# Attention's gate projection on four column groups, and rotations of keys and queries one job later

## The chip, the cores and the metric

The kernel runs on one core of one Trainium2 chip. The metric is the device time of one execution in microseconds (us). Before the change the median of three runs is 1970.93 us (1968.88 to 1974.15).

## The reference, cut to what matters

Two layers of a hybrid model over 512 tokens of width 1024, all in fp32. Each layer normalises the tokens, multiplies them by one wide matrix, and feeds the pieces to three branches (attention with compressed, selected and window keys; a spatial gating unit; a state space model, S5), which are gated, summed and mixed. Then comes a mixture of 32 experts. What the change touches are the 24 columns of attention's gates and the rotary positions:

```python
h = rms_norm(x, norm_mix_g[l])
parts = jnp.split(h @ w_in[l], split_points, axis=-1)
q, k_c, v_c, k_s, v_s, k_w, v_w, nsa_g, sgu_in, s5_in, branch_g = parts     # nsa_g: 24 columns
nsa_gates = jax.nn.sigmoid(nsa_g.astype(jnp.float32)).reshape(B, S, G, R, 3)
...
q_rot = partial_rope(q, positions)
k_slc = partial_rope(k_slc, positions)
k_win = partial_rope(k_win, positions)
...
return gb[..., 0:1] * o_c + gb[..., 1:2] * o_s + gb[..., 2:3] * o_w          # gb: the gates of a block
```

## The kernel before, in words

Each layer is written out as one block with a hand-ordered program for each engine; engines meet through semaphores. A layer has three stages: the projections with S5 (some 145 us), attention with the branch gates and the mixing (some 355 us), and the experts (some 470 us).

TensorE's program of the first stage, in order (line numbers are the profile's):

- Four token jobs `token_job(t)` (L599), one for each tile of 128 tokens: 8 fp32 matmuls of 128x512, the spatial gating unit's input. Every fp32 matmul stands in the trace as two instructions, each with its own weight load, so a job is 16 of them. After job 1 come `nsa_job(0)` and `nsa_job(1)`, after jobs 2 and 3 come `nsa_job(2)` and `nsa_job(3)` (L591): the 24 gate columns of a token tile, 8 matmuls with the tile of `hT` (the turned, normalised tokens) as 128x128 stationary operand and 24 moving columns of `wnsa`. ScalarE takes the sums as tanh (L1134, `nsa_g`).
- Feature jobs (`feature_job`, L585): 24 matmuls of 128x512 in a single-pass type, fp32 split in a high and a low part (`h_hi`, `h_lo`, `w_hi`, `w_lo`): 8 of high by high, 8 with the weights' low part, 8 with the tokens' low part. Jobs J_S5 (2), J_KC (2), then J_KS (2) and J_Q (4), counted `u` = 0 to 5 from J_KS. Then `value_job` (L609) for u = 6 and 7, then `hidden(0)` and `hidden(1)` (L709). A job n needs its bank free (`proj_free`).
- Between them S5: transposes (L633), `taps` (L642, four column groups of 32 columns, `tile_position=(0, r)`), `s5_input` (L652) whose sums VectorE twists, `s5_within` (L662) at u = 1, `s5_output` (L671, four column groups) at u = 2 and 4.
- `rotate(n)` (L701) at the end of step u = n + 1, n = 0 to 5: one fp32 128x512 matmul that multiplies the raw keys or queries by the rotation matrix. It writes banks that `s5_input` had filled, so rotations 0 and 1 wait until VectorE has read those (`twist_read` 2, L1472 of the second half); rotation n >= 2 waits for `rope_done` n - 1. VectorE's `rope(n)` (L1502 to L1507) makes the rotated rows; `hidden(i)` waits for `rope_done` 5 + i.

VectorE's program beside it: S5's parameters and powers, `low_tokens(t)` (L1398, makes `h_lo`, in the place of `hT`, so after `nsa_job(t)`), `split_lo` (L1411, the weights' low parts), the norm of the spatial gating unit, `s5_half(0)`, one `split_lo`, `s5_half(1)` (L1469 to L1492), then `rope(0)` to `rope(5)` with one `split_lo` after `rope(1)`, then S5's first output (L1519) and the next `split_lo`. The SyncE queue loads one slab of weights for every two jobs, each when `proj_done` says that its place is free.

Of the kernel before, what the change touches and what calls it, by code (L numbers as in the profile page):

```python
# [22 lines left out]
ALU = mybir.AluOpType  # L23
ACT = mybir.ActivationFunctionType
AX = mybir.AxisListType.X

P = 128
D = 1024
S = 512
L = 2  # L30
NT = S // P
ND = D // P
# [38 lines left out]
O_V = 41984  # L71
# [9 lines left out]
O_SMALL = O_ROPE + 1024  # L81
O_BBT = O_SMALL + N_SMALL
# [27 lines left out]
def build(nc, io):  # L110
    ctx = ExitStack()
    with ctx:
        def sem(name):
            return ctx.enter_context(nc.semaphore(name))
# [19 lines left out]
        def view(off, *dims):  # L134
            n = int(np.prod(dims))
            if O_BRANCH <= off < O_CONST:
                a = branch[:, off - O_BRANCH:off - O_BRANCH + n]
            elif off < O_XN:
                a = x_place[:, off:off + n]
            elif off < O_HT:  # L140
                a = xn_place[:, off - O_XN:off - O_XN + n]
            elif off < O_SLAB:
                a = hT_place[:, off - O_HT:off - O_HT + n]
            elif off < O_GATE:
                a = slabs[:, off - O_SLAB:off - O_SLAB + n]
            else:
                to = off - O_GATE - (N_BRANCH if off >= O_CONST else 0)
                a = arena[:, to:to + n]
            if len(dims) == 1:
                return a  # L150
            names = "abcd"[:len(dims)]
            return a.rearrange("p (" + " ".join(names) + ") -> p " + " ".join(names),
                               **{k: v for k, v in zip(names[1:], dims[1:])})
# [69 lines left out]
        rope_cos = view(O_ROPE, S)  # L223
        rope_sin = view(O_ROPE + S, S)
        small = {k: view(O_SMALL + a, n) for k, (a, n) in SMALL.items()}
        wnsa = view(O_SMALL + SMALL["wnsa"][0], ND, 24)
        st = O_STAT
        mag = view(st, 8)
        cos1 = view(st + 8, 8)
# [115 lines left out]
        def scale_tokens(dve, g, weighted):  # L345

            for t in range(NT):
                one = slice(t, t + 1)
                dve.wait_ge(g["sq"], t + 1)
                nc.vector.tensor_scalar(sumsq[:, one], sumsq[:, one], 1.0 / D, EPS, ALU.mult, ALU.add).then_inc(g["var"], 1)  # L350
                dve.wait_ge(g["sd"], t + 1)
                nc.vector.reciprocal(rstd[:, one], rstd[:, one]).then_inc(g["rstd"], 1)
                dve.wait_ge(g["rstd"], t + 1)
                scaled(t, weighted).then_inc(g["xn"], 1)
# [6 lines left out]
        def turn_tokens(pe, g):  # L361

            for t in range(NT):
# [4 lines left out]
        over_names = ("ov_shift", "ov_weights", "ov_sel", "ov_gathered", "ov_xe", "ov_gu", "ov_selw", "ov_selT",  # L368
                      "ov_silu", "ov_hid", "ov_hT", "ov_hT_read", "ov_selT_read", "ov_down", "ov_y", "ov_back", "ov_added",
                      "turn_sq", "turn_var", "turn_sd", "turn_rstd", "turn_xn", "turn_saved")  # L370
        so = {n: sem(n) for n in over_names}
        over_sems = list(so.values())
        turn_g = {n: so["turn_" + n] for n in ("sq", "var", "sd", "rstd", "xn")}
        pro_x = [s["pro_x0"], s["pro_x1"], s["pro_x2"], s["pro_x3"]]
        slab_in = [sem("slab_in0"), sem("slab_in1")]
        x_saved = sem("x_saved")

        def half_slab(l, k):

# [7 lines left out]
        with nc.Block() as block:  # L387
            @block.sync
            def _(sp):
                sp.dma_start(pos_i, io["positions"].to_broadcast([P, S])).then_inc(s["pro_in"], 16)  # L390
                sp.dma_start(cst, io["consts"]).then_inc(s["pro_in"], 16)
                for t in range(NT):
                    sp.dma_start(x[:, t, :], io["x"][0, t * P:(t + 1) * P, :]).then_inc(pro_x[t], 16)
                a0, n = SMALL["gmix"]
                for l in range(L):
                    sp.dma_start(gmix[:, 8 * l:8 * l + 8], io["small"][l, :, a0:a0 + n]).then_inc(s["pro_gmix"], 16)
                sp.dma_start(view(slab[0], SLAB), io["dense"][0, 0]).then_inc(slab_in[0], 16)
                sp.dma_start(half_place(1), half_slab(0, 1)).then_inc(slab_in[1], 16)
                sp.wait_ge(s["pro_gmix"], 16 * L)

            @block.tensor
            def _(pe):
                pe.wait_ge(s["pro_in"], 32)
                turn_tokens(pe, turn_g)

            @block.vector
            def _(dve):
                dve.wait_ge(s["pro_in"], 32)
                n = 0

                def link(ins):
                    nonlocal n
                    ins.then_inc(s["pro_dve"], 1)
                    n += 1
                    dve.wait_ge(s["pro_dve"], n)
                link(nc.vector.tensor_copy(rr, pos_i))
                link(nc.vector.tensor_scalar(ang, rr, freq, None, ALU.mult))
                reduce_angle(nc, link, ang, kk, rr, r2)
                scale_tokens(dve, turn_g, False)

            @block.scalar
            def _(act):
                act.wait_ge(s["pro_in"], 32)
                nc.scalar.activation(sumsq[:, 0:1], ident[:, 0:1], ACT.Sqrt).then_inc(s["pro_table"], 1)
                act.wait_ge(s["pro_table"], 1)
                square_tokens(act, turn_g, pro_x)
                act.wait_ge(s["pro_dve"], 2 + N_REDUCE)
                nc.scalar.activation(rope_sin, rr, ACT.Sin).then_inc(s["pro_act"], 1)
                nc.scalar.activation(rope_cos, r2, ACT.Sin).then_inc(s["pro_act"], 1)
                act.wait_ge(s["pro_act"], 2)  # L430
# [16 lines left out]
        s.update({n: sem(n) for n in names})  # L447
        slab_in.append(s["slab_in2"])
        w_in_sem = [[s["we0g"], s["we0u"], s["we0d"]], [s["we1g"], s["we1u"], s["we1d"]]]
        layer_sems = [s[n] for n in names]  # L450


        for layer in range(L):
# [15 lines left out]
            with nc.Block() as block:  # L469
# [82 lines left out]
                def _(pe):  # L552
# [26 lines left out]
                    def feature_job(n, k0, c):  # L579

                        out = bank_p(n)
                        for k in range(GATE_MM):
                            halves_ready(k0 - 1, k)
                            w, h = parts_of(k0)[k // ND]
                            last = nc.tensor.matmul(out, w[:, k % ND, c * P:(c + 1) * P], h[:, k % ND, :], start=(k == 0), stop=(k == GATE_MM - 1))  # L585
                        last.then_inc(s["proj_done"], 1)

                    def nsa_job(t):

                        for k in range(ND):  # L590
                            last = nc.tensor.matmul(ps[:, BANK_S[0], t * 24:(t + 1) * 24], hT[:, k, t * P:(t + 1) * P], wnsa[:, k, :],  # L591
                                                    start=(k == 0), stop=(k == ND - 1))
                        last.then_inc(s["nsa_done"], 1)

                    def token_job(n, w, lo, hi, t):
# [26 lines left out]

                    for c in range(2):
                        feature_job(J_S5 + c, 1, c)
                    for c in range(2):
                        feature_job(J_KC + c, 2, c)
                    pe.wait_ge(s["nsa_read"], 1)
# [85 lines left out]
                    for u in range(1, 10):  # L713
                        if u < 6:
                            feature_job(J_KS + u, S_KS + u // 2, u % 2)
                        elif u == 6:
                            for t in range(2):
                                value_job(t)
                        elif u == 7:
                            for t in range(2, NT):  # L720
                                value_job(t)
                        elif u == 8:
                            pe.wait_ge(s["planes_clear"], 2)
                            hidden(0)
                        elif u == 9:
                            hidden(1)
                        if u == 1:
                            pe.wait_ge(s["ysT_evac"], 2)
                            for J in range(2):
                                s5_within(J)  # L730
                        if 1 <= u <= 6:
                            rotate(u - 1)
                        if u in (2, 4):
                            s5_output(u // 2 - 1)

# [349 lines left out]
                def _(act):  # L1085
# [45 lines left out]
                                nc.scalar.activation(h_hi[:, :, u * P:(u + 1) * P], hT[:, :, u * P:(u + 1) * P], ACT.Identity).then_inc(s["h_hi_ready"], 1)  # L1131
                            split_hi(t + 1)
                    act.wait_ge(s["nsa_done"], NT)
                    nc.scalar.activation(nsa_g.rearrange("p t c -> p (t c)"), ps[:, BANK_S[0], 0:NT * 24], ACT.Tanh, scale=0.5).then_inc(s["nsa_read"], 1)  # L1134
                    act.wait_ge(s["proj_free"], J_SGU + NT)
                    for t in range(NT):
                        ins = nc.scalar.activation(vn[:, t, :], z[:, t, 256:512], ACT.Square, accum_out=vsumsq[:, t:t + 1])
# [16 lines left out]
                    act.wait_ge(s["vvar_ready"], 1)  # L1154
                    nc.scalar.activation(vrstd, vsumsq, ACT.Sqrt).then_inc(s["vsd_ready"], 1)
                    s5_evac(1)
                    act.wait_ge(s["planes_clear"], 2)
                    kc_evac(0)
                    split_hi(S_KS + 1)
# [1067 lines left out]
```

## Time and profile before

| what | value |
|---|---|
| median of 3 runs | 1970.93 us |
| the profiled execution | 1967.01 us |
| its span, first to last instruction | 1965.3 us |
| TensorE busy | 1899.9 us, 97% of the span |
| VectorE busy | 945.9 us, 48% |
| ScalarE busy | 431.4 us, 22% |
| GpSimd busy | 99.4 us, 5% |
| mean granted TensorE clock | 0.989 |

The profiled execution is 3.92 us below the median of the runs, 0.2%. A matmul's time in the trace is from its start to its modelled end, and matmuls overlap, so what an instruction costs is read from the distance between starts. Idle time of TensorE and what ended it stands in brackets in the timeline.

### The profile page before, as it was taken

Reading aid. Unit: us, or ns where it says so; the run is one execution under the profiler, and the core shown is the slowest. Engines: PE = TensorE matmul, PEld = TensorE weight load, DVE = VectorE, ACT = ScalarE, POOL = GpSimd, SP = SyncE. Lnnn points to the kernel's source line nnn. Section 1 sums busy time; section 2 is a strip of 40 time slices with the busy share of each in tenths; the row PEclk is TensorE's granted clock in tenths of the full one; section 3 lists DMA queues with packets and bytes.
Section 4 is the critical chain, followed back from the end, with each engine's and each line's share of the span. In section 5 each row is a group of like instructions: output and inputs, shape, how many; then the busy total and the mean of one; then the engine's idle time right before and its main releaser. Section 6 shows DMA issues by size and latency. Waiting matters only on the chain. (4 is left out here: it accounts for less than half of the span.)

```text
span 1965.3 us, 26006 instructions
## 1 busy us (share of the span) xinstructions
PE 1899.9 (97%) x10104; PEld 1122.1 (57%) x10105; DVE 945.9 (48%) x1875; ACT 431.4 (22%) x816; POOL 99.4 (5%) x205
## 2 busy tenths in 40 slices
PE   6999999999999999999899999999999999999995
PEld 4868777645554454454357877775465455455442
DVE  7754555345443443443478455553363343343344
ACT  4413444102211111111233244440121111111112
POOL 4500000000000000000063000000000000000000
PEclk9999999999999999999999999999999999999998
DMA  4222112333699999999722221132528999999993
GB/s 165 65 92 86 65 63 67 129 107 157 266 425 426 425 429 426 425 426 426 321 70 65 92 73 68 54 105 89 216 91 338 426 427 423 428 430 422 423 428 156
DMA packets 56398, 482.10 MB, mean 245 GB/s; under 512 B 9584, under 2 KB 22384, under 8 KB 27376
## 3 DMA queue, kind: packets, MB, share of 16 engines
q1 hardware_dynamic: 56304, 480.80, 60.4%
q8 instruction: 64, 1.05, 0.2%
q14 instruction: 30, 0.25, 0.0%
HBM read 476.59 MB, written 4.19 MB: 245 GB/s over the span
## 5 line engine op out<-in xcount | busy, mean ns | idle before, releaser
L1756 DVE TENSOR_TENSOR x_tokens<-x_tokens,ps 128x512 f32<-128x512 f32 x240 | 161.7, 687 | 236.9 <-PE ps L990 236.0
L1056 PE MATMUL ps<-arena,branch 128*64 128x512 f32 x512 | 226.6, 595 | 0.0
L1056 PE MATMUL ps<-slabs,branch 128*64 128x512 f32 x512 | 226.6, 595 | 0.0
L1006 PE MATMUL ps<-slabs,arena 128*64 128x512 f32 x512 | 225.0, 592 | 0.7 <-issue 0.7
L1006 PE MATMUL ps<-arena 128*64 128x512 f32 x512 | 225.0, 592 | 0.1
L1007 PE MATMUL ps<-arena 128*64 128x512 f32 x512 | 225.1, 592 | 0.0
L1007 PE MATMUL ps<-slabs,arena 128*64 128x512 f32 x512 | 225.0, 592 | 0.0
L749 PE MATMUL ps<-h_hi,w_parts 128*128 128x512 f32 x768 | 210.8, 408 | 1.5 <-DVE w_parts L1411 1.5
L749 PEld LDWEIGHTS ps<-h_hi,w_parts 128*128 128x128 f32 x768 | 135.1, 189 | 38.8 <-issue 9.2
L1006 PEld LDWEIGHTS ps<-slabs,arena 128*64 128x64 f32 x512 | 70.1, 137 | 146.0 <-issue 145.9
L1006 PEld LDWEIGHTS ps<-arena 128*64 128x64 f32 x512 | 70.0, 137 | 144.8 <-issue 144.8
L1056 PEld LDWEIGHTS ps<-arena,branch 128*64 128x64 f32 x512 | 67.5, 137 | 133.5 <-issue 133.5
L1265 ACT ACTIVATE branch<-ps 64x512 f32<-64x512 f32 x64 | 37.8, 591 | 391.9 <-PE ps L1007 391.9
L1800 DVE SCALAR_TENSOR_TENSOR split_rows<-ps,arena,split_rows 128x512 fp32r<-128x512 f32 x64 | 48.1, 751 | 157.2 <-ACT split_rows L1275 157.2
L1762 DVE TENSOR_TENSOR branch<-ps,branch 64x512 f32<-64x512 f32 x64 | 44.1, 688 | 163.5 <-ACT branch L1265 162.5
L978 PE MATMUL ps<-split_rows,h_lo 128*128 128x256 f32 x448 | 115.4, 281 | 0.0
L980 PE MATMUL ps<-split_rows,x_lo 128*128 128x256 f32 x448 | 115.2, 281 | 0.0
L1275 ACT ACTIVATE split_rows<-ps,arena 128x512 fp32r<-128x512 f32 x64 | 44.0, 687 | 309.3 <-PE ps L1056 309.3
L989 PE MATMUL ps<-split_rows 128*128 128x512 f32 x240 | 105.6, 440 | 4.9 <-DVE x_tokens L1756 4.9
L749 PE MATMUL ps<-h_lo,w_parts 128*128 128x512 f32 x384 | 108.1, 406 | 0.0
L1411 DVE TENSOR_TENSOR w_parts<-slabs,w_parts 128x512 fp32r<-128x512 f32 x144 | 96.0, 730 | 11.2 <-ACT w_parts L1123 10.7
L990 PE MATMUL ps<-split_rows 128*128 128x512 f32 x240 | 94.5, 394 | 0.0
(346 smaller groups left out, 2972.5 us busy)
## 6 DMA issues: line engine op xcount, KB each, us to landing
arena<-in_expert_w_gate SPq DMA_DIRECT2D x32, 2048.0 KB, 12.4
arena<-in_expert_w_up SPq DMA_DIRECT2D x32, 2048.0 KB, 16.8
arena<-in_expert_w_down SPq DMA_DIRECT2D x32, 2048.0 KB, 9.8
slabs<-in_expert_w_gate SPq DMA_DIRECT2D x32, 2048.0 KB, 15.4
slabs<-in_expert_w_up SPq DMA_DIRECT2D x32, 2048.0 KB, 19.9
slabs<-in_expert_w_down SPq DMA_DIRECT2D x32, 2048.0 KB, 14.1
slabs<-in_gate_w SPq DMA_DIRECT2D x24, 1024.0 KB, 4.8
slabs<-in_dense SPq DMA_DIRECT2D x10, 2048.0 KB, 8.1
```

The source lines that it names most:

```text
L749: last = nc.tensor.matmul(fill.out, wp[:, k % ND, (n % 2) * P:(n % 2 + 1) * P], hp[:, k % ND, :], start=(k == 0), stop=(k == GATE_MM - 1))
L978: nc.tensor.matmul(ps[:, bank + part // 4, col:col + QUAD], x_hi[:, t, d * P:(d + 1) * P], sel[:, t, :], start=(t == 0), stop=False)
L980: last = nc.tensor.matmul(ps[:, bank + part // 4, col:col + QUAD], x_lo[:, t, d * P:(d + 1) * P], sel[:, t, :], start=False, stop=(t == NT ...
L989: nc.tensor.matmul(out, to, y_hi[:, cols], start=True, stop=False)
L990: nc.tensor.matmul(out, to, y_lo[:, cols], start=False, stop=True).then_inc(s["back_done"], 1)
L1006: nc.tensor.matmul(ps[0:64, BANK_GU[b], :], xk, low[:, k, :], start=(k == 0), stop=(k == ND - 1), tile_position=(0, 0))
L1007: return nc.tensor.matmul(ps[64:P, BANK_GU[b], :], xk, high[:, k, :], start=(k == 0), stop=(k == ND - 1), tile_position=(0, 64))
L1056: done = nc.tensor.matmul(ps[64 * b:64 * b + 64, BANK_Y[half], :], hidT[:, k, CAP * b:CAP * (b + 1)], w_down[b][:, k, half * 512:(half + 1 ...
L1411: v.tensor_tensor(w_lo[k][:, part], view(slab[k], SLAB // 2)[:, part], w_hi[k][:, part], ALU.subtract)\
L1756: v.tensor_tensor(xs, xs, ps[:, BANK_BACK[n % 2], :], ALU.add).then_inc(s["back_added"], 1)
L1762: v.tensor_tensor(hid[rows], ps[other, BANK_GU[b], :], silu[rows], ALU.mult).then_inc(s["hid_done"], 1)
L1800: v.scalar_tensor_tensor(y_lo[:, cols], ps[:, BANK_Y[half], :], w_slot, y_hi[:, cols], ALU.mult, ALU.subtract).then_inc(s["y_lo_ready"], 1)
```

## The change

The gate weights become the stationary operand, 32 columns of them at a time (24 and the 8 that follow in memory; 8 zeroed columns follow the last), and the tokens move. Chunk k of the contraction goes to column group k % 4, so four partial sums of the gates stand in four partition groups of the bank. ScalarE copies the bank to `nsa_parts` (in the place of `v_tok`). After the two S5 jobs `nsa_sums` multiplies each token tile of it by `stack`, a 128x24 matrix of four stacked identities made once in the prologue, which adds the four parts and turns them back to tokens on partitions; ScalarE takes tanh from there, after `s5_evac(1)`. `rotate(n)` moves from step u = n + 1 to u = n + 2. The new wait uses a semaphore of the overflow program, and the two ranges of semaphores are cleared together.

```diff
-        wnsa = view(O_SMALL + SMALL["wnsa"][0], ND, 24)
+        w0 = SMALL["wnsa"][0]
+        wnsa = [view(O_SMALL + w0 + 24 * k, 32) for k in range(ND)]
+        nsa_end = view(O_BBT, 8)
+        stack = view(O_BBT + 8, 24)
+        nsa_parts = view(O_V, S)
...
                 scale_tokens(dve, turn_g, False)
+                link(nc.vector.memset(nsa_end, 0.0))
+                link(nc.vector.tensor_tensor(stack, ident[:, 0:24], ident[:, 32:56], ALU.add))
+                link(nc.vector.tensor_tensor(stack, stack, ident[:, 64:88], ALU.add))
+                link(nc.vector.tensor_tensor(stack, stack, ident[:, 96:120], ALU.add))
...
-        layer_sems = [s[n] for n in names]
+        layer_sems = over_sems + [s[n] for n in names]
+
+        shared = dict(nsa_parted="ov_silu")
+        s.update({n: so[of] for n, of in shared.items()})
...
                     def nsa_job(t):
 
                         for k in range(ND):
-                            last = nc.tensor.matmul(ps[:, BANK_S[0], t * 24:(t + 1) * 24], hT[:, k, t * P:(t + 1) * P], wnsa[:, k, :],
-                                                    start=(k == 0), stop=(k == ND - 1))
+                            r = 32 * (k % 4)
+                            last = nc.tensor.matmul(ps[r:r + 32, BANK_S[0], t * P:(t + 1) * P], wnsa[k], hT[:, k, t * P:(t + 1) * P],
+                                                    start=(k < 4), stop=(k >= 4), tile_position=(0, r))
+                        last.then_inc(s["nsa_done"], 1)
+
+                    def nsa_sums():
+
+                        pe.wait_ge(s["nsa_parted"], 1)
+                        for t in range(NT):
+                            last = nc.tensor.matmul(ps[:, BANK_S[1], t * 24:(t + 1) * 24], nsa_parts[:, t * P:(t + 1) * P], stack, start=True, stop=True)
                         last.then_inc(s["nsa_done"], 1)
...
                     for c in range(2):
                         feature_job(J_S5 + c, 1, c)
+                    nsa_sums()
                     for c in range(2):
                         feature_job(J_KC + c, 2, c)
...
-                        if 1 <= u <= 6:
-                            rotate(u - 1)
+                        if 2 <= u <= 7:
+                            rotate(u - 2)
...
                     act.wait_ge(s["nsa_done"], NT)
-                    nc.scalar.activation(nsa_g.rearrange("p t c -> p (t c)"), ps[:, BANK_S[0], 0:NT * 24], ACT.Tanh, scale=0.5).then_inc(s["nsa_read"], 1)
+                    nc.scalar.activation(nsa_parts, ps[:, BANK_S[0], :], ACT.Identity).then_inc(s["nsa_parted"], 1)
...
                     s5_evac(1)
+                    act.wait_ge(s["nsa_done"], NT + 1)
+                    nc.scalar.activation(nsa_g.rearrange("p t c -> p (t c)"), ps[:, BANK_S[1], 0:NT * 24], ACT.Tanh, scale=0.5).then_inc(s["nsa_read"], 1)
```

## Rows read from the trace of the kernel before

**Rows 1.** Waits of TensorE, whole span: us in total, times, longest.
```profile
PE ps L701 <- DVE arena L1472: 7.9, 2, 4.0
```
**Rows 2.** Windows: the experts' stage of layer 0 (columns: engines' busy us, clock, DMA share, GB/s).
```profile
520.00:990.00 470.00, 460.28 (x2337) 225.93 (x2336) 186.28 (x264) 57.93 (x108) 0.00 (x0) 0.99 0.97 409
```
**Rows 3.** Timeline of TensorE (start, us, instructions), layer 0, gate and S5 jobs.
```profile
35.35 3.65 PE L591 MATMUL ps<-arena,hT 128*128 128x24 f32 x32
38.84 7.11 PE L599 MATMUL ps<-slabs,hT 128*128 128x512 f32 x16
...
54.44 1.86 PE L591 MATMUL ps<-arena,hT 128*128 128x24 f32 x16
56.14 3.88 PE L585 MATMUL ps<-h_hi,w_parts 128*128 128x512 f32 x16
...
61.67 3.79 PE L585 MATMUL ps<-h_hi,w_parts 128*128 128x512 f32 x16
```
**Rows 4.** Line L591 in both layers: ns min/median/max, first and last start.
```profile
L591 PE MATMUL ps<-arena,hT x128: 186/269/270, 35.3 to 1026.6; 128*128 128x24 f32 x128
```
**Rows 5.** Timeline of TensorE, layer 0, steps u = 1 to 4.
```profile
98.56 4.51 PE L662 MATMUL ps<-branch,arena 32*32 32x512 f32 x64
107.02 2.04 PE L701 MATMUL ps<-xn_tokens,arena 128*128 128x512 f32 x2 [3.95 <-DVE arena L1472]
...
116.29 1.02 PE L701 MATMUL ps<-xn_tokens,arena 128*128 128x512 f32 x2
117.24 1.94 PE L671 MATMUL ps<-arena 128*32 128x127 f32 x64
119.11 3.94 PE L585 MATMUL ps<-h_hi,w_parts 128*128 128x512 f32 x16
...
124.71 1.02 PE L701 MATMUL ps<-xn_tokens,arena 128*128 128x512 f32 x2
...
131.05 1.02 PE L701 MATMUL ps<-xn_tokens,arena 128*128 128x512 f32 x2
```
**Rows 6.** Timeline of VectorE, layer 0, the tokens' low parts.
```profile
51.55 2.81 DVE L1411 TENSOR_TENSOR w_parts<-slabs,w_parts 128x512 fp32r<-128x512 f32 x4
56.44 1.42 DVE L1398 TENSOR_TENSOR h_lo<-hT,h_hi 128x1024 fp32r<-128x1024 f32 x1 [2.07 <-PE ps L591]
```
**Rows 7.** Timeline of ScalarE, layer 0: the first S5 and KC evacuations.
```profile
61.88 1.13 ACT L1097 ACTIVATE branch<-ps 128x512 f32<-128x512 f32 x1 [3.26 <-PE ps L585]
...
72.81 2.46 ACT L1097 ACTIVATE arena<-ps 64x512 f32<-64x512 f32 x4 [4.38 <-PE ps L585]
```
**Rows 8.** Timeline, start of layer 0: VectorE's first work after the prologue.
```profile
20.10 4.87 DVE L1329 TENSOR_TENSOR hT<-ps,arena 128x512 f32<-128x512 f32 x8 [1.95 <-PEq L387]
```
**Rows 9.** Windows, layer 0 and layer 1, after the wait (columns as in rows 2).
```profile
110.00:111.00 1.00, 1.00 (x4) 0.71 (x3) 1.00 (x3) 0.00 (x0) 0.00 (x0) 0.50 0.00 0
1080.00:1081.00 1.00, 1.00 (x4) 0.81 (x3) 1.00 (x2) 0.00 (x0) 0.00 (x0) 0.50 0.00 0
```
**Rows 10.** Timeline of TensorE, layer 1, rotations 0 and 1.
```profile
1077.61 1.10 PE L701 MATMUL ps<-xn_tokens,arena 128*128 128x512 f32 x2 [3.95 <-DVE arena L1472]
...
1085.67 1.02 PE L701 MATMUL ps<-xn_tokens,arena 128*128 128x512 f32 x2
```
**Rows 11.** Timeline of VectorE, layer 0: S5's scans and the first rope.
```profile
92.30 0.69 DVE L1469 TENSOR_TENSOR arena<-ps,arena 128x512 f32<-128x512 f32 x1 [2.73 <-PE ps L652]
...
106.19 0.69 DVE L1472 TENSOR_TENSOR arena<-ps,arena 128x512 f32<-128x512 f32 x1
...
114.06 0.69 DVE L1502 TENSOR_TENSOR arena<-ps,arena 128x512 f32<-128x512 f32 x1
```
**Rows 12.** Timeline of VectorE, layer 0: the last rope and S5's output.
```profile
147.20 0.69 DVE L1502 TENSOR_TENSOR arena<-ps,arena 128x512 f32<-128x512 f32 x1 [4.46 <-PE ps L701]
...
149.38 1.53 DVE L1519 SCALAR_TENSOR_TENSOR branch<-branch,arena,ps 128x512 f32<-128x512 f32 x2
```
**Rows 13.** Timeline of TensorE, layer 0: the hidden layers.
```profile
152.68 10.39 PE L709 MATMUL ps<-arena,slabs 128*128 128x93 f32 x64
```

More of the change, by code:

```diff
@@ L370, in build @@
                       "turn_sq", "turn_var", "turn_sd", "turn_rstd", "turn_xn", "turn_saved")
+        pro_x = [s["pro_x0"], s["pro_x1"], s["pro_x2"], s["pro_x3"]]
+        slab_in = [sem("slab_in0"), sem("slab_in1")]
+        x_saved = sem("x_saved")
         so = {n: sem(n) for n in over_names}
@@ L373, in build @@
         turn_g = {n: so["turn_" + n] for n in ("sq", "var", "sd", "rstd", "xn")}
-        pro_x = [s["pro_x0"], s["pro_x1"], s["pro_x2"], s["pro_x3"]]
-        slab_in = [sem("slab_in0"), sem("slab_in1")]
-        x_saved = sem("x_saved")
         def half_slab(l, k):
```

## The prediction

> **What bounds the kernel now.** I read the page's busy shares first, then TensorE's waits, then the windows by stage, then the timelines of TensorE, VectorE and ScalarE through the projections of both layers. TensorE is busy 97% of the span, so a microsecond of its work that goes, or of its waiting, is a microsecond of the kernel unless something else catches it. The reader is to see in the list of waits that one wait stands out inside the layers: rotation 0 waits twice, 4.0 us each, for VectorE's twist [rows 1]. In the experts' stage the DMA engines are 97% busy beside a TensorE that is 98% busy (460.28 of 470) [rows 2]; but the first expert's transfers are issued only when the merge, TensorE's and VectorE's own work, is done, so this stage starts earlier by whatever the stages ahead of it save, and is no shorter. In the timelines one sees that TensorE's jobs of the projections stand edge to edge apart from that wait.
>
> **The gate jobs.** Before: 32 instructions from 35.35 to 38.84 are 3.49 us, and 16 from 54.44 to 56.14 are 1.70 [rows 3]; the third run of them, of 16 again, lasts 1.70 too. Sum 6.89 us in a layer, 108 ns an instruction, which moves only 24 columns: the weight load of 128 columns sets the pace. After: as many instructions (64 in a layer), each a load of 32 columns and 128 moving ones, on four column groups in turn. The nearest row is `s5_output`, 128x32 stationary, 127 moving columns, fp32, four column groups in turn: 64 instructions from 117.24 to 119.11, 1.87 us, 29.2 ns each [rows 5]. It is the same shape but for one column, so I take 64 x 29.2 = 1.87 us. Leaving the groups costs a little: the feature job behind that row takes 119.11 to 124.71, 5.60, the one behind the last gate job 56.14 to 61.67, 5.53 [rows 3, 5]. So 0.07 for each of the three runs, 0.21. New cost 2.08, saved 4.81. The other bound: the groups run one after the other. The token job moves 512 columns in 16 instructions from 38.84, by its record of 7.11 us some 434 ns each, so 128 columns take 108 ns [rows 3], 6.9 us for the 64, and nothing is saved.
>
> The Trainium skill speaks against this edit in one point: "TensorEngine Tiling (Array Packing)", section "Key Properties", says that a change of tiling mode drains TensorE. Three runs in and out are six such changes in a layer. The rows put leaving at 0.07 us. If each change emptied the engine for the 269 ns of a gate instruction [rows 4] it would be 1.6 us in a layer, and the forecast below some 2 us later in all. The other sentences do without this.
>
> **What catches a part of it.** The first feature job needs the tokens' low part of all four tiles for its last 8 matmuls. Before, VectorE waited 2.07 us for the last gate job and then made it from 56.44 to 57.86 [rows 6]. The work ahead of it (51.55 plus 2.81) ends at 54.36, and that doesn't move, since VectorE is not waiting there. So the low part is there at 54.36 + 1.42 = 55.78 at the earliest. TensorE starts the feature job at 56.14 - 4.81 = 51.33 and wants it after 16 of its 24 matmuls, 3.7 us later, at 55.0. It waits some 0.75. What is left is 4.81 - 0.75 = 4.06, say 4.0 us.
>
> **The sums.** `nsa_sums` is 4 fp32 matmuls, 8 instructions of the old gate jobs' shape (128x128 stationary, 24 moving): 8 x 108 = 0.87 us, with 0.1 for the change of type between two single-pass jobs. It waits for ScalarE's copy of 512 columns. ScalarE stands idle 3.26 us before the first S5 evacuation [rows 7], the copy is some 0.4 us longer than the tanh it replaces, and TensorE has two feature jobs, 11 us, in between: nothing. The tanh now stands behind the root of the norm, which uses another function table, so a table load moves there; queued behind it are the KC evacuations, before which ScalarE is idle 4.38 us [rows 7]; the load taken there spares one at S5's gelu. Were that cover gone, it would be 1.3 us a layer. The net of the gates: 4.0 - 0.97 = 3.0 us in a layer. The whole chain of VectorE and ScalarE behind follows TensorE or is ahead of it. Line L591 looks the same in both layers (one median, 269 ns, no spread) [rows 4], so 6.0 for the two. Bounds: -1.2 a layer (serial groups and the sums), +3.9 (no catch, no 0.1).
>
> **The rotations.** Before, TensorE ends `s5_within` at 103.07 and starts rotation 0 at 107.02: 3.95 idle [rows 5], in layer 1 as well [rows 10]. The idle time also costs clock: behind it the granted clock is 0.50, 1.2 GHz, in both layers [rows 9]. Rotation plus feature job take 124.71 to 131.05 = 6.34 at the full clock, but 107.02 to 116.29 = 9.27 here [rows 5] and 1077.61 to 1085.67 = 8.06 in layer 1 [rows 10]: 2.93 and 1.72 lost. After the change the feature job of u = 2 stands in the gap. Its banks and weights are ready (its weights' low part was split before the scans). Rotation 0 then comes at 98.56 + 4.4 + 5.6 = 108.6 in old times against a twist that is read at 106.87 (106.19 + 0.68) [rows 5, 11]: 1.7 us to spare. Both ends hang on TensorE's `s5_input`, since VectorE waits for it at 92.30 [rows 11], so the gates' saving moves both and takes nothing from this margin. Saved: 3.95 + 2.93 + 3.95 + 1.72 = 12.55, less 0.1 a layer for the change of mode that the idle time used to hide: 12.35. Bounds: 0 (the wait returns with its clock), 12.6.
>
> What each later step meets: rope 0 starts at 114.06 [rows 11] as before, because VectorE is in the scans until then, and rotation 2 (a whole step later than before against rope 0) needs only that. `s5_output(1)` wants the second scan, which is done just before 114.06, and comes some 9 us after that. The weights' low part for the value jobs is split after rope 1, which waits for a rotation now one job later; the value jobs are more than two jobs on. At the end, rotation 5 stands after the last value job, directly ahead of the hidden layers. Rope 5 and S5's output take VectorE 147.20 to 150.91, 3.7 us [rows 12]. `hidden(1)` needs rope 5 (2.2 us) after 5.2 us of `hidden(0)`; the glu behind needs the gelu after 10.39 us of hidden layers [rows 13] and a feature job. 3 us to spare at the tighter one; if that cover were gone, a late rope 5 would cost at most its own 2.2 us a layer. SyncE's slabs wait on `proj_done` of jobs, no order in its queue changes, and no job is moved against another.
>
> **Elsewhere.** The prologue's four small VectorE instructions (estimate 0.2 us each, 0.8) lie in the 1.95 us in which VectorE waits for the last transposes [rows 8]. The wider clear is still one instruction between two barriers. Nothing.
>
> **Sum.** 6.0 + 12.35 = 18.3 us. The profiled execution would go from 1967.01 to 1948.7; by the median of the runs, 3.92 above it, 1970.93 - 18.3 = 1952.6. I forecast the latter.
>
> **Rivals.**
> (a) The column groups don't overlap at this shape: the gates lose 1.2 a layer instead of gaining 3.0. 18.3 - 8.4 = 9.9, so 1961.0. Against it: the s5_output row, same shape.
> (b) The wait comes back at a later reader of VectorE (rotation 0 with its margin of 1.7 us, rotation 2, hidden 1), as long and with its dip of the clock. Then only the gates' 6.0 remain: 1964.9; with half of it back, 1958.8. For it: VectorE is solid from 92.30 to 114.06. Against it: each margin above.
> (c) The experts' weights run on a clock of their own, being 97% of the DMA time, and the gain vanishes there: 1970.9. Against it: the first transfer hangs on the merge.
> (d) The other side: the three gate runs and the sums, short and with small waits around them (the 0.75 us for the low part), drop the clock each time as the wait of 3.95 did. One mechanism, at four places a layer, 2.9 us each: 23 us lost against 18.3 gained, 1975.6. It decides from seven such dips on. Against it: `s5_output` and the taps, in the same form, stand in stretches at the full clock, and the only dips here follow an idle engine of some 4 us.
>
> **How the numbers follow.** Forecast 0.80, (a) 0.05, (b) 0.09, (c) 0.03, (d) 0.03. The forecast's own spread is 1948 to 1957: 2.6 from the runs' scatter, 2 from the mode changes and the low part. To leave out no more than 2 in 10 the range takes in (a) and part of (b): 1946 to 1962. About 0.3%, 5.9 us, is what a measurement can tell from no change: at most 1965.0 counts as faster. The forecast, (a) and nearly all of (b) are faster, 0.93; (c) and the rest of (b) are the same, 0.04; (d) is slower, 0.03.
>
> **What would show it.** L591 with 128x32 weights and 16 instructions in some 0.5 us; the first feature job with a wait of under 1 us for VectorE's L1398; 8 instructions of 0.87 us behind the S5 jobs; no wait at L701 and no stretch at clock 0.50 near 105 us and 1075 us; the hidden layers start some 9.5 us earlier in layer 0 (3.0 + 6.8) and the expert loops as long as before. Wrong: a wait of over 1 us at L701, L709 or L585; gate instructions 100 ns apart; a longer expert stage.

## The result, and the profile after

The changed kernel takes 1952.03 us (median of 4 runs, 1951.81 to 1954.24), the kernel before 1971.2 (4 runs, 1968.88 to 1974.15): a ratio of 0.9905, interval 0.9887 to 0.9922. That is 19.2 us by the medians, against 18.3 forecast and a forecast time of 1952.6. The two profiled executions are only 14.9 apart: 1967.01 (span 1965.3) and 1952.09 (span 1950.4). What the 4 us between these two differences come from is one of the questions of the experiments.

TensorE's timeline of the gates in layer 0, the answer to [rows 3]:

```profile
35.46 1.08 PE L603 MATMUL ps<-hT,arena 128*32 128x128 f32 x32
36.47 7.13 PE L618 MATMUL ps<-slabs,hT 128*128 128x512 f32 x16
43.54 0.65 PE L603 MATMUL ps<-hT,arena 128*32 128x128 f32 x16
44.11 7.13 PE L618 MATMUL ps<-slabs,hT 128*128 128x512 f32 x16
51.18 0.65 PE L603 MATMUL ps<-hT,arena 128*32 128x128 f32 x16
51.75 3.92 PE L596 MATMUL ps<-h_hi,w_parts 128*128 128x512 f32 x16
55.52 2.10 PE L596 MATMUL ps<-h_lo,w_parts 128*128 128x512 f32 x8
57.46 3.79 PE L596 MATMUL ps<-h_hi,w_parts 128*128 128x512 f32 x16
61.08 1.98 PE L596 MATMUL ps<-h_lo,w_parts 128*128 128x512 f32 x8
62.90 0.96 PE L611 MATMUL ps<-arena 128*128 128x24 f32 x8
63.70 2.57 PE L596 MATMUL ps<-h_hi,w_parts 128*128 128x512 f32 x10
```

From start to start, 32 gate instructions take 1.01 us and each 16 take 0.57. The first feature job starts at 51.75 instead of 56.14. The sums are the 0.80 us from 62.90 to 63.70.

TensorE around the rotations, the answer to [rows 5]: no idle time stands in brackets any more.

```profile
95.25 4.51 PE L682 MATMUL ps<-branch,arena 32*32 32x512 f32 x64
99.69 3.94 PE L596 MATMUL ps<-h_hi,w_parts 128*128 128x512 f32 x16
103.47 1.98 PE L596 MATMUL ps<-h_lo,w_parts 128*128 128x512 f32 x8
105.29 1.02 PE L721 MATMUL ps<-xn_tokens,arena 128*128 128x512 f32 x2
106.24 1.94 PE L691 MATMUL ps<-arena 128*32 128x127 f32 x64
108.11 3.94 PE L596 MATMUL ps<-h_hi,w_parts 128*128 128x512 f32 x16
...
141.68 1.02 PE L721 MATMUL ps<-xn_tokens,arena 128*128 128x512 f32 x2
142.54 10.39 PE L729 MATMUL ps<-arena,slabs 128*128 128x93 f32 x64
```

The hidden layers start at 142.54 instead of 152.68 [rows 13], 10.1 us earlier, and last 10.39 as before. In TensorE's list of waits (total, times, longest) the rotation is gone, the answer to [rows 1]:

```profile
PE ps L363 <- DVE arena L347: 18.3, 3, 13.9
PE ps L618 <- DVE hT L1351: 8.0, 2, 6.1
PE ps L1009 <- DVE x_tokens L1778: 4.9, 12, 0.7
PE ps L936 <- DVE arena L1713: 3.4, 2, 1.7
```

The experts' stage is no shorter and no longer: TensorE is busy 460.63 us in a window of 470, with DMA at 0.97, as in [rows 2].

```profile
510.00:980.00 470.00, 460.63 (x2338) 225.93 (x2336) 185.60 (x262) 57.97 (x108) 0.00 (x0) 0.99 0.97 409
```

One row did grow, and nothing in the change touches it. At the seam between the layers VectorE evacuates the turned tokens to `hT`. It was idle for 5.53 us ahead of that before; it is idle for 7.99 after, and both rows name TensorE's queue (PEq) as what ended the idle time. First before, then after:

```profile
989.27 4.88 DVE L1329 TENSOR_TENSOR hT<-ps,arena 128x512 f32<-128x512 f32 x8 [5.53 <-PEq L2113]
```

```profile
982.14 4.88 DVE L1351 TENSOR_TENSOR hT<-ps,arena 128x512 f32<-128x512 f32 x8 [7.99 <-PEq L2135]
```

The whole difference of the profiled pair, by positions before and after: up to `s5_within` of layer 0 −3.3 (98.56, 95.25); rotations of layer 0 −6.8; hidden layers to the last turn of the tokens +0.5; the seam +2.5; layer 1 up to `s5_within` −2.9 (78.44 us from the first token job, then 75.52); rotations of layer 1 −5.6 (52.91, then 47.28); the rest +0.8. Sum −14.9. The +0.5 and the +0.8 were not traced to a cause.

### The profile page after: what moved, and what is told of

Its sections match the earlier page's. It is cut to its first block and busy times, and to the rows that moved or that the text cites. A ratio compares the mean times of both kernels' runs of the same rounds, so it can differ in the third digit from the quotient of the medians.

```text
span 1950.4 us, 26047 instructions
## 1 busy us (share of the span) xinstructions
PE 1891.5 (97%) x10120; PEld 1108.5 (57%) x10121; DVE 943.5 (48%) x1879; ACT 435.5 (22%) x820; POOL 102.7 (5%) x205
## 6 DMA issues: line engine op xcount, KB each, us to landing
slabs<-in_expert_w_up SPq DMA_DIRECT2D x32, 2048.0 KB, 19.6
```

## The experiments

Three questions were open. Where does the seam's +2.5 come from: theory A, the wider clear of the semaphores, or theory C, the place of TensorE's code behind the layer, which the change shifts? Why do the medians differ by 4 us more than the profiled pair: do the old gate jobs let TensorE's clock fall in some executions (theory E)? And do the two edits earn what the sum gave each of them, with the margin that it gave?

**e1_clear, the wider clear alone.** On the kernel before:

```diff
-        layer_sems = [s[n] for n in names]
+        layer_sems = over_sems + [s[n] for n in names]
```

> The kernel before with one part of the change alone: the overflow program's 23 semaphores are cleared together with the layer's 121 between the layers (144 in one clear). Theory A (the wider clear costs what the seam of the changed kernel shows: VectorE idle there 7.99 us against 5.53, and 0.6 us more of slow first jobs in layer 1): 3.1 us slower than before, idle of VectorE at the seam near 8.0. Theory B (the seam's length comes from something else in the change): as before, idle 5.5.

Measured: 1971.97 us (12 runs) against 1970.76 (18), ratio 1.0002, interval 0.9992 to 1.0012; the seam's idle time is 5.02. A fell. The profiled run of this kernel, at 1973.93, shows something else, on a program whose gates and tokens are those of the kernel before:

```profile
35.38 4.18 PE L591 MATMUL ps<-arena,hT 128*128 128x24 f32 x32
39.38 9.97 PE L599 MATMUL ps<-slabs,hT 128*128 128x512 f32 x16
49.19 1.86 PE L591 MATMUL ps<-arena,hT 128*128 128x24 f32 x16
```

The token job behind the first run of gate jobs lasts 9.97 us where [rows 3] have 7.11. The window of that microsecond (engines' busy time, then granted clock, DMA share, GB/s) has the clock at 0.50, 1.2 GHz, with TensorE busy throughout:

```profile
40.00:41.00 1.00, 1.00 (x2) 0.34 (x1) 0.93 (x3) 0.00 (x0) 0.84 (x3) 0.50 0.00 0
1014.00:1015.00 1.00, 1.00 (x2) 0.34 (x1) 0.97 (x2) 0.00 (x0) 0.92 (x2) 0.50 0.00 0
```

Layer 1 has the same (the second window). From the first to the second run of gates it takes 13.80 us there (1008.40 to 1022.20), where the profiled execution before took 10.44 (1005.96 to 1016.40). Twice 3.4 is 6.7 of the 6.9 us between 1973.93 and 1967.01.

The mean granted clock, which is known of every execution, goes the same way. Of 42 further executions of the kernel before, the three at 0.989, the value of the profiled one, took 1966.16 to 1966.65 us; the 17 at 0.987 took 1969.38 to 1972.08, and the two at 0.985 took 1975.49 and 1975.71. By arithmetic one such stretch, 6.8 us long at half the clock, lowers the mean by 0.002.

**e2_narrow, the changed kernel without the wider clear.** The copy's mark goes on a semaphore that was cleared anyway, and its later readers count to 2:

```diff
-        layer_sems = over_sems + [s[n] for n in names]
+        layer_sems = [s[n] for n in names]
...
-                        pe.wait_ge(s["nsa_parted"], 1)
+                        pe.wait_ge(s["nsa_read"], 1)
```

> The changed kernel with the clear of before (121 semaphores): the new wait counts on nsa_read, 1 for the copied parts and 2 for the tanh. Theory A: 3.1 us faster than the changed kernel, near 1949.0 where before is 1971.2, seam 5.5 us. Theory B: as the changed kernel, 1952.

Measured: 1952.29 (1950.84 to 1953.04, 6 runs), ratio 0.9906, interval 0.989 to 0.9922; seam 8.42. The same as the changed kernel. The wider clear costs nothing on either side, and the seam stays long. The experiments below build on this kernel.

**e3_rotate, the rotations alone,** on the kernel before:

```diff
-                        if 1 <= u <= 6:
-                            rotate(u - 1)
+                        if 2 <= u <= 7:
+                            rotate(u - 2)
```

> The kernel before with the rotations one step later and nothing else. By the forecast's working 12.35 us faster than before: 3.95 of waiting in each layer, 2.93 and 1.72 of slow clock, less 0.1 each. Rival (the margin of 1.7 us against VectorE's twist depends on the shorter gate jobs): a wait of over 1 us at the rotations is left, gain under 10.

Measured: 1956.77 (1954.05 to 1961.11, 6 runs), ratio 0.9935, interval 0.9916 to 0.9953: 14.0 us less (the interval is 9 to 17). The wait and its stretch at 0.50 are gone, and the seam's idle time is 4.58. The trace gives the edit more closely than the medians: from `s5_within` to the hidden layers it is 47.28 us in both layers, where it was 54.12 and 52.91, so 6.84 and 5.63, together 12.5 against the 12.35 of the forecast. The rival fell.

**e4_gates, the gates alone,** with the narrow clear and the rotations where they were (the diff is that of the change without the `rotate` lines, plus e2's).

> The gates on column groups alone, with the clear and the rotations of before. The forecast says 3.0 us a layer, the trace of the changed kernel 3.3 to 3.4: 6.0 to 6.8 us faster than before, with the wait of 3.95 us at rotation 0 back in both layers and the clock at 0.50 behind it. Rival (one part's gain depends on the other): the two alone don't sum to the changed kernel with the narrow clear.

Measured: 1963.15 (1962.27 to 1964.92, 7 runs), ratio 0.9961, interval 0.9946 to 0.9976: 7.6 us less, with a seam of 8.11. The wait at rotation 0 is what it was:

```profile
95.30 4.51 PE L680 MATMUL ps<-branch,arena 32*32 32x512 f32 x64
103.76 2.04 PE L719 MATMUL ps<-xn_tokens,arena 128*128 128x512 f32 x2 [3.95 <-DVE arena L1492]
```

It is 3.95 us to the digit, though everything ahead of it comes 3.3 us earlier. That is the step "both ends hang on `s5_input`". The 7.6 is above the 6.0 to 6.8 expected, and is itself a sum: 6.8 of gate work less, some 3 lost at the longer seam, and some 3.4 that the median of before spends on a stretch at half the clock (an inference, see below) make 7.2. The two single gains add to 21.6, the change brings 19.2; the intervals of the two (4 and 3 us to either side) don't tell that from a plain sum.

**e5_pad18, never-run code,** on the kernel before: 36 more waits in each layer's TensorE program for overflowing experts, which these inputs never enter (the expectation counts two waits as one instruction, hence its 18):

```diff
-                                    pe.wait_ge(so["ov_sel"], 1)
+                                    for _ in range(37):
+                                        pe.wait_ge(so["ov_sel"], 1)
```

> The kernel before with 18 more TensorE instructions a layer (36 waits that hold at once) in the overflow program, which is not run: they only move the place of what follows in TensorE's program, by as many instructions as the new gates add. Theory C (the seam between the layers, VectorE's idle of 5.5 us before and 8.0 to 8.4 in every kernel with the new gates, hangs on where TensorE's next block lies in its program): idle 8.0 or more at the seam, 2.5 us slower. Rival D (the seam hangs on something that the new gates do): 5.5 or less, time as before.

Measured: 1974.87 (12 runs) against 1971.03 (17), ratio 1.0016, interval 1.0006 to 1.0025. The seam of the kernel before, with nothing changed that runs:

```profile
992.60 2.48 DVE L1329 TENSOR_TENSOR hT<-ps,arena 128x512 f32<-128x512 f32 x4 [7.76 <-PEq L2114]
```

7.76 us instead of 5.02 to 5.53, 3.8 us slower (by the interval 1 to 5) where 2.5 was expected. That is C: the seam hangs on the code's size or place. In this execution the clock also fell behind the gate jobs in layer 1, and not in layer 0:

```profile
1014.88 9.79 PE L599 MATMUL ps<-slabs,hT 128*128 128x512 f32 x16
```

**e6_pad238, the same on e2** with 476 waits more a layer (238 by the count of e5), to see whether the effect comes back to its old value after 256 instructions.

> The changed kernel with the narrow clear and 238 more instructions that are not run, so that with the 18 of the gates TensorE's code of the next layer is moved by 256 instructions of 64 bytes, one piece of 16384 bytes as the trace's instruction transfers have them. Theory C: the seam is back at 5.5 us, 2.5 to 3 us faster than that kernel, near 1949.5 where before is 1971. Rival D: as it, 1952.3.

Measured: 1952.72 (1950.8 to 1953.99, 4 runs), ratio 0.9906, interval 0.9891 to 0.992; seam 8.39. With this pad the seam doesn't come back.

**e11_cut, less never-run code,** on e2: the overflow program's gather leaves out its products with the tokens' low part, 32 matmuls in a layer, which these inputs never reach:

```diff
-                                    expert_gather(nc, ps, 2, (x_hi, x_lo), ov_sel).then_inc(so["ov_gathered"], 1)
+                                    expert_gather(nc, ps, 2, (x_hi,), ov_sel).then_inc(so["ov_gathered"], 1)
```

> The changed kernel (clear as before) with 32 TensorE instructions fewer in each layer's program for overflowing experts, which doesn't run with these inputs: its gather leaves out the products with the low part of the tokens. No instruction that runs is changed. Theory (the seam between the layers hangs on where TensorE's code behind it lies): with fewer instructions than the kernel before has, the seam's VectorE idle goes back to 4.6 to 5.6 us from 8.4, and the time to 1949.5 us (2.5 to 3 less). Rival (the seam hangs on something that the changed kernel does ahead of it, as its waits and clears, and only by chance followed the pad): 8.4 and 1952.3. Between them (another alignment, no simple rule): a seam between 4.6 and 8.4.

Measured: 1947.96 (1946.46 to 1949.07, 4 runs), ratio 0.9883, interval 0.9866 to 0.9899. It is 4.3 us faster than e2 and the fastest of all; not one instruction that runs is different. The seam:

```profile
978.40 0.69 DVE L1349 TENSOR_TENSOR hT<-ps,arena 128x512 f32<-128x512 f32 x1 [4.47 <-PEq L2133]
```

4.47 instead of 8.42. A little of that goes again in the token jobs behind: from the end of VectorE's last instruction ahead of the seam to the first gate job it is 22.39 us here and 25.94 in e2, so 3.55 of the 4.3. C holds in both directions. For inputs that overflow this kernel would not be the whole computation, so it shows where the time lies and is no replacement as it stands.

**e7_onegroup, the column groups,** on e2: all eight chunks in column group 0, accumulated there, and the copy and the sums over its 32 rows alone.

```diff
-                            r = 32 * (k % 4)
+                            r = 0
...
-                                                    start=(k < 4), stop=(k >= 4), tile_position=(0, r))
+                                                    start=(k == 0), stop=(k == ND - 1), tile_position=(0, r))
```

> The changed kernel with the narrow clear, all eight chunks of the gates' contraction in column group 0, and the sums over 32 partitions with the plain identity. Forecast's rival (a) priced the groups one after the other at 108 ns an instruction: then 4.9 us a layer slower than on four groups, some 9.8 in all, 1962, with gate instructions 108 ns apart. If the small weight load alone made the gain, they stay near 29 ns apart and the time is the same, 1952.

Measured: 1961.9 (1960.97 to 1962.55, 5 runs), ratio 0.9952, interval 0.994 to 0.9965: 9.6 more than e2.

```profile
35.47 3.68 PE L601 MATMUL ps<-hT,arena 128*32 128x128 f32 x32
39.08 7.13 PE L616 MATMUL ps<-slabs,hT 128*128 128x512 f32 x16
```

3.61 us for 32 is 113 ns each. In four groups it is 1.01 for 32, some 32 ns each. So it is the groups side by side that make the gain, and not the small weight load alone. One record lasts 273 ns either way: how many run beside each other is seen from start to start, not in the mean duration. The clock stays at full speed here, although these instructions, each moving 128 columns, come as slowly as the old ones.

**e8_double, the old gate jobs twice,** on the kernel before:

```diff
-                        for k in range(ND):
+                        for k in [*range(ND), *range(ND)]:
```

> The kernel before with each old gate job done twice. By count 6.9 us a layer, 13.8 in all. Theory E (the old gate jobs, 24 columns behind each weight load, let the clock fall in some executions, as in the profiled execution of the clear-only kernel at 39 us and 1012 us, and this is why the runs of kernels with the old gates spread over 7 to 9 us and those with the new over 2 to 3): doubled they do so in most executions, 16 to 24 us slower than before, and the profile shows the clock at 0.50 in the token jobs. Rival F (the spread has nothing to do with them): 13.8 slower, no dip there.

Measured: 2000.47 (2000.19 to 2001.82, 4 runs), ratio 1.0148, interval 1.0133 to 1.0162: 29.4 us more. By count 128 instructions more at 108 ns would be 13.8.

```profile
35.93 9.80 PE L591 MATMUL ps<-arena,hT 128*128 128x24 f32 x64
45.55 9.53 PE L599 MATMUL ps<-slabs,hT 128*128 128x512 f32 x16
```

The clock of the microseconds behind them, and the seam of this kernel:

```profile
45.00:47.00 2.00, 2.00 (x6) 1.36 (x6) 1.91 (x3) 0.00 (x0) 1.77 (x4) 0.50 0.00 0
...
1005.56 4.87 DVE L1329 TENSOR_TENSOR hT<-ps,arena 128x512 f32<-128x512 f32 x8 [9.08 <-PEq L2113]
```

64 at 108 ns are 6.9 us, but it is 9.62 to the next start; the token job behind lasts 9.53 instead of 7.11. The forecast of 16 to 24 was too low, and not all of the 15.6 beyond the count is clock: the seam is 9.08 where it was 5.53, for this kernel too has more TensorE code (theory C), and takes 3.5 of it. For the rest E holds: TensorE, busy all the time with matmuls of 24 moving columns, is granted 0.52 from 40 to 45 us and 0.50 from 45 to 47, and in layer 1 0.50 from 1030 to 1037. All four runs have a mean clock of 0.980 or 0.981, against 0.985 to 0.989 before. The runs scatter accordingly. With the old gates they spread over 8.1 (e1, 12 runs), 7.9 (e5, 12) and 7.1 us (e3, 6), with the new ones over 2.4 (the change, 4), 2.2 (e2, 6) and 2.7 (e4, 7).

**e9_late4 and e10_late8, the margin of the rotations,** on e2: four or eight needless products on VectorE between the two halves of its S5 work, ahead of the second twist, which rotation 0 waits for (the edit is there, and not at the keys' norms, which the expectation names).

```diff
+                            for _ in range(8):
+                                link(v.tensor_tensor(s5_c, rope_sin, rope_cos, ALU.mult))
```

> The changed kernel (clear as before), with four more products on VectorE (about 0.69 us each, 2.8 us in all) issued between the two halves of the feature norms of the keys, so that the twist of the keys and all that VectorE does behind it in its order comes 2.8 us later. Theory: one job of distance left the rotations a margin of 1.7 us (the table that the keys' rotation reads was ready 1.7 us before). So 1.1 us of wait show at the first rotation of each layer, and the time is 1954 to 1956 us; TensorE idles too shortly for the clock to fall. Rival (the distance hides all of VectorE's lateness, because the rotations come late by TensorE's own order): 1952.3, no wait. Rival (VectorE's later work is the path from here on, and every added microsecond shows): 2.8 per layer, 1957.9.

> As the one with four added products, with eight of them, 5.5 us. Theory: 5.5 less the margin of 1.7 gives 3.8 us of wait at the first rotation of each layer, about the wait that the kernel before had there (3.95), +7.6 us: 1960. If such a wait also lets the clock fall, as it did in the kernel before in layer 0 (0.50 in one slice of TensorE behind the rotation), up to 1.5 us a layer more, 1961 to 1963. Rival (every added microsecond shows): +11, 1963.3, with waits of 5.5. Rival (the distance hides it all): 1952.3.

Measured: 1952.99 (1952.2 to 1954.33, 4 runs), ratio 0.9908, interval 0.9891 to 0.9924; and 1962.74 (1962.59 to 1963.64, 4 runs), ratio 0.9957, interval 0.9941 to 0.9974. Four products:

```profile
107.11 1.10 PE L719 MATMUL ps<-xn_tokens,arena 128*128 128x512 f32 x2 [1.17 <-DVE arena L1492]
108.14 1.94 PE L689 MATMUL ps<-arena 128*32 128x127 f32 x64
```

Eight:

```profile
109.81 2.05 PE L719 MATMUL ps<-xn_tokens,arena 128*128 128x512 f32 x2 [4.07 <-DVE arena L1492]
111.79 3.41 PE L689 MATMUL ps<-arena 128*32 128x127 f32 x64
...
120.74 1.02 PE L719 MATMUL ps<-xn_tokens,arena 128*128 128x512 f32 x2
```

The waits are 1.17 and 4.07 where a margin of 1.7 gave 1.1 and 3.8. Behind the wait of 4.07 the rotation lasts 2.05 instead of 1.02 and `s5_output` (L689) 3.41 instead of 1.94: the granted clock is 0.50 from 110 to 114 us. Behind the wait of 1.17 it is 1.00. So the first 2.8 us of lateness cost 0.7 and the next 2.7 cost 9.8, in two layers. In the profiled runs the hidden layers of layer 0 start at 143.01 (e2), 144.42 (e9) and 149.57 (e10), and of the 6.56 between first and last 4.07 are the wait and 2.5 the clock. e10 fell where it was expected (1961 to 1963), e9 missed its 1954 to 1956: four products cost 0.7 in all instead of some 2.3. The waits are there (1.17 and 1.16 in the two layers, hidden layers +1.4 in layer 0), so the margin is right; a difference of 1.6 between two medians is inside their intervals of 3 us to either side.

## Why the prediction was right

The time was forecast within 0.6 us, and that closeness is luck. The two edits did what their steps said, with the sizes that their steps gave within some 0.4 us a layer. But the sum met the median with two misses that cancel: 3.4 us less gained in the profiled pair than forecast, the seam above all, and some 4 us more in the medians than in the pair.

**Gate instructions.** 1.87 us a layer forecast, 1.01 + 0.57 + 0.57 = 2.15 measured, 34 ns an instruction where `s5_output` has 29.2. That row of [rows 5] was near enough, and rival (a) was a fair picture of the other case: e7 measured it at 9.6 us, 8.4 forecast. e7 also shows that it is the groups that overlap.

**Leaving the groups.** 0.07 for each of three runs of gates forecast. The two token jobs behind them take 7.07 from start to start (36.47 to 43.54) where they took 6.95 (38.84 [rows 3] to 45.79 before): 0.12 each, and 0.05 shows in the feature job.

```profile
45.79 1.86 PE L591 MATMUL ps<-arena,hT 128*128 128x24 f32 x16
```

Together that is 0.29 instead of 0.21. The Trainium skill ("TensorEngine Tiling (Array Packing)", "Key Properties") says that a change of mode drains TensorE; the trace shows no more than these 0.12 us for the way back, and nothing that can be told apart for the way in.

**The wait for the low part.** 0.75 forecast, no idle time in the trace. VectorE began it where the prediction had it, right behind its row at 51.50, but it took 1.22 instead of 1.42, so it was ready at 55.46. TensorE wanted it at 55.52, not at 55.0: its first feature job began at 51.75 and not at 51.33, since the gate jobs and the two token jobs behind them took 0.3 more than the sum's 2.08, and the gates began 0.1 later in this execution.

```profile
51.50 2.83 DVE L1433 TENSOR_TENSOR w_parts<-slabs,w_parts 128x512 fp32r<-128x512 f32 x4
54.24 1.22 DVE L1420 TENSOR_TENSOR h_lo<-hT,h_hi 128x1024 fp32r<-128x1024 f32 x1
```

The 8 matmuls took 2.10 instead of 1.98, about 0.1 us late. So this catch was sized some six times too large; it is the term of the gates that was off most.

**Sums and the tables.** 0.97 forecast with the change of type. Measured are 0.80 for the sums, and the feature job behind them takes 5.59 us (63.70 to 69.29) where it took 5.45, so 0.94, with no wait for ScalarE. The table load moved as said, but it spares none at S5's gelu; that load is still there. ScalarE's idle time ahead of the KC evacuation shrank from 4.38 [rows 7] to 3.80, so the cover held:

```profile
64.20 1.28 ACT L1178 ACT_TABLE_LOAD   x1
65.50 0.25 ACT L1178 ACTIVATE arena<-ps 128x96 f32<-128x96 f32 x1
69.55 2.48 ACT L1117 ACTIVATE arena<-ps 64x512 f32<-64x512 f32 x4 [3.80 <-PE ps L596]
...
144.08 1.28 ACT L1206 ACT_TABLE_LOAD   x1
```

**The gates' net.** 3.0 a layer forecast; 3.3 measured in layer 0, with a start 0.1 later, so 3.4: 6.89 less 2.15, 0.29, 0.13 and 0.94. In layer 1 it is 2.9, because the first token jobs took 0.6 longer in this execution (15.25 us, then 15.86), and 3.5 without that.

**Rotations.** 6.78 and 5.57 forecast for the two layers, 6.83 and 5.63 measured. The margin of 1.7 us is 1.72 in the trace, from the end of the twist's last reading instruction (102.89 plus 0.68) to rotation 0 at 105.29:

```profile
102.89 0.68 DVE L1494 TENSOR_TENSOR arena<-ps,arena 128x512 f32<-128x512 f32 x1
```

e9 and e10 confirm it by using it up. Rivals (b) and (c) fell: no later reader of VectorE waits, and the experts' window is the same.

**"Elsewhere nothing" failed.** The step looked for instructions that the change adds outside the two edits. The wider clear is nothing, as e1 and e2 show. But the seam costs 2.5 us more, 3.1 with the slower token jobs behind it, and e5 and e11 show that this hangs on how much code TensorE has or where it lies, run or not; no row of the trace of before could have priced it. Another 1.3 us, the +0.5 and +0.8 of the list above, have no known cause.

**The base of the sum failed in the other direction.** The sum was made against one profiled execution and then set on the median, 3.92 above it, as if these 3.92 were scatter that both kernels have. In the trace of before the gate jobs leave the clock at full speed. In e1's trace the same jobs lower it in both layers, for 3.4 us each. An execution with one such stretch would lie at some 1970.4, which is near the median. Of the four traces with the old gates once, before and e3 have no such stretch, e5 has one and e1 two; the eight traces with the new gates have none. So the median gained some 4 us that the profiled pair doesn't show. That e1's and e5's stretches are there, and that doubling the jobs brings them, is shown; that the median of before contains one is inferred from these numbers, the spread, and the clocks of the 42 executions. With that the medians come out by parts: rotations 12.5, gates 6.8, the seam −3.1 and a stretch 3.4 are 19.6, and 19.2 were measured. Rival (d) was right that gate jobs can lower the clock, but had it at the wrong kernel: it is the old ones that do. Its "the only dips here follow an idle engine of some 4 us" held for the one trace and not for the kernel.

## What to carry to other kernels

In this kernel a small product that loads 128 columns of weights to move 24 costs twice: 108 ns an instruction, and a clock that falls behind it in some executions. Turned round, on four column groups, it costs 32 to 36 ns, and no trace has the clock fall there. A wait can be hidden by moving its reader one job later. How safe that is, the margin tells: the time from the end of what is waited for to the start of the reader, read from both engines' timelines. Here it was 1.7 us, and once it was used up 2.7 us of lateness cost 9.8. When the profiled execution and the median lie apart, ask what in the other runs is slower before putting a sum on the median.

## What the runs showed that was not expected

- Code that is never entered changes the time of the seam between the layers. VectorE's idle time there, with TensorE's queue as releaser, was 4.47 us with less of such code (e11) and 4.58 to 5.53 with TensorE's code as long as before (before, e1, e3). It was 7.20 to 8.42 with the new gates (with e6's pad 8.39), 7.76 with e5's pad and 9.08 with the doubled gates, whose added code does run. It looks like a step between two levels. From the start of the idle time to the first gate job it is 22.2 to 23.1 us at the lower level and 25.3 to 25.9 at the upper (27.3 in e8), so the step is worth some 3 us at the one seam of this kernel. The traces show where the added time lies. 1.9 to 2.5 us after the end of TensorE's last matmul ahead of the seam an instruction transfer of 16 KB (queue 8) starts, in each of the 13 traces: at 988.95 before, at 979.44 after, and each lasts some 1 us. In the four traces with the short seam VectorE goes on 0.3 to 0.4 us after its start, before it has ended (989.27 before); in the nine with the long seam it goes on 1.5 to 2.3 us after its end (982.14 after). The DMA rates of before from 984 to 990 us and of after from 975 to 983 us, in 40 slices each, show it: the 109 of the first, the 164 of the second, there with two transfers of 8 KB beside it:

```profile
GB/s 0 0 0 0 0 0 0 0 0 0 0 0 0 0 0 0 0 0 0 0 0 0 0 0 0 0 0 0 0 0 0 0 0 109 0 55 0 0 55 0
GB/s 0 0 0 0 0 0 0 0 0 0 0 0 0 0 0 0 0 0 0 0 0 0 164 0 0 0 0 0 0 0 0 0 0 0 0 0 0 0 0 0
```

That fits a TensorE which has its next code already in the one case and waits for it in the other, but no run changes the transfer by itself, so what the queue waits for stays open.
- TensorE that is 1.00 busy isn't safe from the half clock. Behind 32 instructions of 24 columns the granted clock is 0.50 in one trace (e1) and 1.00 in another of the same instructions (before); behind 64 of them it is 0.50 (e8, 45 to 47 us). Instructions of 128 columns at the same pace (e7, 113 ns) left it at full speed.
- An idle TensorE of 1.17 us left the clock alone, and one of 3.95 or 4.07 halved it.
